# Shifting the start addresses of the low rows of a split-precision transformer block in on-chip memory

## The chip, the cores and the metric

The kernel runs on one core of a Trainium2 chip. A core has five engines that run their own instruction streams and meet at semaphores: TensorE (PE, matrix products; its weight loads are the rows PEld), VectorE (DVE), ScalarE (ACT), GpSimd (POOL) and SyncE (SP), which issues the transfers here. Operands lie in the on-chip memory as 128 partitions by a number of bytes; an address below is the byte offset inside every partition. Products go to eight accumulation banks (PS). The metric is the device time of one execution in microseconds (us), median of several.

## The reference, cut to what matters

Two layers of a hybrid block over 256 tokens `x` and, in layer 0 alone for the outputs, 256 context tokens. Width is 1024, feed-forward width 2816, everything float32.

```python
for l in range(DEPTH):
    # h, hc: x and context after rmsnorm and modulation
    p = h @ w_in[l]; pc = hc @ w_in[l]          # 13 parts: conv a, q k v, recurrent, conv d, gates
    ys = (short_conv(..) @ w_a_out, window_attention(..) @ w_b_out,
          (gelu(r_g) * rglru(..)) @ w_c_out, conformer_conv(..) @ w_d_out)
    x = x + gt1 * (sum(sigmoid(gl) * ys) @ w_out)
    gate, up = split(modulate(rmsnorm(x)) @ w_ffn_in)
    x = x + gt2 * ((silu(gate) * up) @ w_ffn_out)
    # the context tokens go the same way in layer 0 alone
return rmsnorm(x) * g_final
```

## The kernel before

**Split operands.** Nearly every product is made of three. A float32 matrix is held as a rounded part (type fp32r) and a low part (what the rounding left out). For each weight tile of 128x128 and each row tile of activations the helper `products` makes rounded weight times rounded row, rounded weight times low row, and low weight times rounded row, into one bank. So a third of the products stream a low row, and two of three load a rounded weight.

**Where things lie.** `build` allocates one tensor after another with `sb`, each starting at a multiple of 32 bytes. Rounded weights are WH and low weights WL (two slabs each, eight pairs of tiles in a slab). There are two pairs of row tensors. HH and HL (rounded and low) hold the normed input of the block, and later the hidden rows that the second feed-forward product reads (`H` and `FZ` in the code). ZH and ZL hold the branch values of the block (`Z`), and the normed input of the first feed-forward product (`FH`). A row tile k of 512 tokens begins at k * 2048 bytes; 8 * 516 words are reserved for HH and HL, because the helper `unscaled_slab` keeps rows of 258 columns in them, which begin at k * 2064 bytes plus 1032 for the second set of tokens. Of the small tensors, SG and SM hold softmax statistics, AMP, SELB, LC and BD2 small vectors. RAW receives the weight slabs from memory; S, CD, TMP, G and PADA are working rows, and SR, TMPR and PADAR are the same bytes as S, TMP and PADA with the rounded type (the attention uses them).

Bytes modulo 256 at which the tensors begin before: X, WH, WL, ZH, ZL, HH and HL at 0; S, CD, RAW, TMP and G at 128; PADA at 0.

**Order of the work.** Stages follow `STAGES`: c_in, kv, q, d_in, c_out, b_out, a_cu, a_b, a_out, d_out, w_out, and then three times ff_in and ff_out. In each, TensorE takes slabs in turn (`slab`), each once its low weight is made, and its bank pair is emptied. In layer 0 a product has 512 columns, in layer 1 mostly 256. SyncE loads a slab to RAW, ScalarE rounds it to WH, and GpSimd (some by VectorE) subtracts to WL. The instruction before each product loads its own 128x128 tile as weights, also where the same tile was just used.

```python
            def products(s, t, z, w, k, nk=KC):
                zh, zl, at = z
                out = bank(2 * s + t, w)
                a = s * SLAB + k * 2 * P + t * P
                wh, wl = WH[:, a:a + P], WL[:, a:a + P]
                mm(out, wh, row(zh, k, w, at), k == 0, False)
                mm(out, wh, row(zl, k, w, at), False, False)
                return mm(out, wl, row(zh, k, w, at), False, k == nk - 1)
```

Of the kernel before, what the change touches and what calls it, by code (L numbers as in the profile page):

```python
# [24 lines left out]
KC = D // P  # L25
# [144 lines left out]
def build(nc, stream, modw, lruw, xT, cT, prm, rope, consts, outT):  # L170
    with ExitStack() as ctx:
        def sb(name, n, dt=F32):
            return ctx.enter_context(nc.sbuf_tensor(name, [P, n], dt))
# [11 lines left out]
        WH = sb("WH", 2 * SLAB, F32R)  # L185
        WL = sb("WL", 2 * SLAB, F32R)
        ZH = sb("ZH", KC * NT, F32R)
        ZL = sb("ZL", KC * NT, F32R)
        HH = sb("HH", KC * UROW, F32R)
        AMP = sb("AMP", 2 * 2 * KC)  # L190
        SELB = sb("SELB", 32)
        LC = sb("LC", 2 * 16)
        HL = sb("HL", KC * UROW, F32R)
        S, SR = sb_and_rounded("S", KC * NT)
        CD = sb("CD", KC * NT)
# [6 lines left out]
        CST = sb("CST", 5 * P + 2)  # L202
        CIN = sb("CIN", 2 * KC)
        SILC = sb("SILC", 32 * KC + 30)
        SG = sb("SG", 2 * KC)
        LT = sb("LT", 5 * 16)
        EPST = sb("EPST", 2)
        WARM = sb("WARM", 1)
        BD2 = sb("BD2", KC)
        SM = sb("SM", 3 * 14)  # L210
        PS = ctx.enter_context(nc.psum_tensor("PS", [P, 8, 512], F32))

        HB = LT[:, 32:64]
# [5 lines left out]
        def tmp(i, a=0, b=NT):  # L219
            return TMP[:, i * NT + a:i * NT + b]  # L220
# [23 lines left out]
        def lru(n, j, w=NT):  # L244

            if n == KC - 1 and j in (0, 2):
                return row(CD, KC - 2 + j // 2, w)
            return (ALT[j] if n % 2 else S[:, j * NT:(j + 1) * NT])[:, 0:w]
# [9 lines left out]
        def par(l, name, i=0, n=1):  # L258

            return PRM[:, ds(i + (l * NPRM + _cols[name]), n)] if not isinstance(i, int) else \  # L260
                PRM[:, l * NPRM + _cols[name] + i:l * NPRM + _cols[name] + i + n]

        def row(t, j, w=NT, a=0):

            return t[:, j * NT + a:j * NT + a + w] if isinstance(j, int) else t[:, ds(j * NT + a, w)]

        def urow(t, k, c, w=NX, a=0):

            at = k * UROW + c * (NX + 2) + a
            return t[:, at:at + w]  # L270
# [9 lines left out]
        def ubank(t, c, w=NX, a=0):  # L280

            return PS[:, ((4, 6), (5, 1))[t][c], a:a + w]
# [9 lines left out]
        def normed(nm):  # L292
            return (HH, HL) if nm == "n1" else (ZH, ZL)

        def lc(j, n, d):

            return LC[:, ds(n + (16 * j + 8 * d), 1)]

# [4 lines left out]
        def bank(b, w=NT, a=0):  # L303
            return PS[:, b, a:a + w]

        def seqs(ap, c):

            return ap.rearrange("p (c t) -> p c t", c=c)
# [281 lines left out]
        def _(pe):  # L590
            def mm(out, lhs, rhs, start, stop):
                return nc.tensor.matmul(out, lhs, rhs, start=start, stop=stop)  # L592
# [102 lines left out]
            def mod_columns(q, size, out):  # L695

                pe.wait_ge(mod_copied, q + 1)
                for t in range(2):
                    last = mm(out[:, :, 2 * t:2 * t + 2], MROW[q % 2][:, t * P:(t + 1) * P], SELB[:, 0:2 * size], True, True)
                last.then_inc(mod_cols, 1)  # L700

            def unit_columns(j):
# [4 lines left out]
                for g in range(4):  # L707
                    last = nc.tensor.matmul(PS[32 * g:32 * g + 32, 4, 0:n // 4], SELB[:, 0:32],
                                            ACROSS[:, at:at + n].rearrange("p (x g) -> p g x", g=4)[:, g],
                                            start=True, stop=True, tile_position=(0, 32 * g))  # L710
                last.then_inc(mod_cols, 1)

            H, Z, Z2 = (HH, HL, 0), (ZH, ZL, 0), (ZH, ZL, NX)
            FH, FZ = (ZH, ZL, 0), (HH, HL, 0)

            def unscaled_slab(m, l):
# [4 lines left out]
                for k in range(KC):  # L721
# [5 lines left out]
                    for t in range(2):  # L727
                        wh, wl = weights_of(0, t, k)
                        for c in vectors:
                            out = ubank(t, c, NX + 2)  # L730
                            mm(out, wh, urow(HH, k, c, NX + 2), k == 0, False)
                            mm(out, wh, urow(HL, k, c, NX + 2), False, False)
                            last = mm(out, wl, urow(HH, k, c, NX + 2), False, k == KC - 1)
                        if k == KC - 1:
# [104 lines left out]
            for l in range(DEPTH):  # L839
# [30 lines left out]
                for c in range(NT // P):  # L870
                    out = PS[:, 2 + c // 2, (c % 2) * 2 * P:(c % 2 + 1) * 2 * P]
                    for k in range(KC):
                        w0 = SLAB + k * 2 * P
                        h0 = k * NT + c * P
                        mm(out, HH[:, h0:h0 + P], WH[:, w0:w0 + 2 * P], k == 0, False)
                        mm(out, HH[:, h0:h0 + P], WL[:, w0:w0 + 2 * P], False, False)
# [144 lines left out]
        def _(act):  # L1021
            def fn(out, in_, f, **kw):
                return nc.scalar.activation(out, in_, f, **kw)  # L1023
# [8 lines left out]
            def tiles(m, s, t=1):  # L1032
                act.wait_ge(tile_done[s], 2 * m + (t + 1))
# [134 lines left out]
            act.wait_ge(in_loaded, 16)  # L1168
            fn(SG[:, :], CIN[:, :], ACT.Sigmoid).then_inc(sigmoid_c, 1)
            act.wait_ge(par_loaded, 32)  # L1170
# [14 lines left out]
            for l in range(DEPTH):  # L1185
# [50 lines left out]
                def z_high(n):  # L1236
                    act.wait_ge(a["ci_r"].sem, a["ci_r"].at(n, "y"))
                    fn(row(ZH, n, W), lru(n, 5, W), ACT.Copy).then_inc(a["ci_h"].sem, 1)

# [44 lines left out]
                def gate(which, at=0):  # L1284
                    def body(n, s, m):
                        fn(tmp(at + s, 0, W), bank(2 * s, W), ACT.Sigmoid).then_inc(a[which + "_a"].sem, 1)
                    return body
# [36 lines left out]
                def probs(n, u):  # L1324
                    sm = 14 * u
                    act.wait_ge(dv.sem, dv.at(n, f"n{u}"))
                    if u < 2:
                        fn(seqs(bank(4 + u), 2) if l and n == 0 else PR[u], seqs(bank(4 + u), 2), ACT.Exp, scale=SCALE, bias=SM[:, sm + 4:sm + 5],
                           accum_out=SM[:, sm + 6:sm + 7]).then_inc(da.sem, 1)
                    else:  # L1330
                        for q in range(2):
                            fn(PR[0][:, q], bank(6, NC, q * NC), ACT.Exp, scale=SCALE,
                               bias=SM[:, sm + 4 + q:sm + 5 + q], accum_out=SM[:, sm + 6 + q:sm + 7 + q]).then_inc(da.sem, 1)
                    act.wait_ge(dv.sem, dv.at(n, f"f{u}"))
                    q = 2 if u == 2 else 1
                    fn(SM[:, sm + 8:sm + 8 + q], SM[:, sm + 8:sm + 8 + q], ACT.Exp).then_inc(da.sem, 1)

# [47 lines left out]
                if l:  # L1385
                    b = pair_base(l, "c_out")
                    act.wait_ge(a["di_z"].sem, a["di_z"].at(KC - 1, "z"))
                    for n in range(KC):
# [4 lines left out]
                        gate("co")(n, s, m)  # L1393
                        fn(row(ZH, n, W, NX), row(CD, n, W), ACT.Copy).then_inc(a["bz_h"].sem, 1)
                else:
# [7 lines left out]
                    for k in range(KC):  # L1403
                        fn(row(ZH, k, W), row(CD, k, W), ACT.Copy).then_inc(a["bz_h"].sem, 1)
                    tiles(b, 1)
# [101 lines left out]
                for f in range(len(FF_PARTS)):  # L1507
# [7 lines left out]
                    def unscaled_in(m):  # L1515
                        tiles(m, 0)
                        for c in range(C):
                            ue = a["un_e"]
                            act.wait_ge(ue.sem, ue.at(0, f"r0{c}"))
                            last = fn(tmp(0, c * NX, (c + 1) * NX), ubank(0, c), ACT.Sigmoid, bias=SM[:, c:c + 1])  # L1520
                        last.then_inc(fa.sem, 1)
# [16 lines left out]
        def _(dve):  # L1538
            V = nc.vector

            def tt(out, x, y, op):
                return V.tensor_tensor(out, x, y, op)  # L1542
# [4 lines left out]
            def ts(out, x, s1, s2, op0, op1=None):  # L1547
                return V.tensor_scalar(out, x, s1, s2, op0, op1) if op1 is not None else V.tensor_scalar(out, x, s1, None, op0)  # L1548
# [86 lines left out]

            def z_low(n, w, src, at=0, zh=ZH, zl=ZL):
                return tt(row(zl, n, w, at), src, row(zh, n, w, at).bitcast(F32), SUB)

            def decay_rates(l):
# [22 lines left out]
                for j, f in enumerate((-4.0, 2.0)):  # L1662
                    ts(LC[:, 16 * j:16 * j + 16], k0, f, None, MUL).then_inc(lv.sem, 1)
                ts(HB, par(l, "ba", 0, 32), 0.5, None, MUL).then_inc(lv.sem, 1)
# [7 lines left out]
            tt(SILC[:, 30:30 + 32 * KC].rearrange("p (k c) -> p k c", c=32)[:, :, 0:2], CIN[:, :].rearrange("p (k c) -> p k c", c=2),  # L1672
               SG[:, :].rearrange("p (k c) -> p k c", c=2), MUL).then_inc(silu_c, 1)
            dve.wait_ge(par_loaded, 32)
            for g in range(1, 4):
                if g > 1:
                    dve.wait_ge(sel_sum, g - 1)
                tt(SELB[:, :], SELB[:, :] if g > 1 else IDENT[:, 0:32], IDENT[:, 32 * g:32 * g + 32], ADD)\
                    .then_inc(*((silu_c, 1) if g == 3 else (sel_sum, 1)))
            for l in range(DEPTH):  # L1680
# [21 lines left out]

                ts(BD2[:, :], par(l, "conv_d_b", 0, KC), 2.0, None, MUL).then_inc(mv.sem, 1)
                def inverse_root(nm, c_all):
# [270 lines left out]
                def scalars(u):  # L1975
                    q = 2 if u == 2 else 1
                    return (SM[:, 14 * u + 2 * j:14 * u + 2 * j + q] for j in range(7))

# [87 lines left out]
                def conv_d(taps):  # L2066

                    sv = a["cd"].sem
                    for i, k in taps:
                        for t in range(2):  # L2070
# [6 lines left out]
                            if k == 0:  # L2077
                                ins = ts(out, padded(j, C, -(TAPS_D // 2)), w, BD2[:, j:j + 1], MUL, ADD)
                            else:
# [66 lines left out]
                for n in range(KC // 2):  # L2146
# [12 lines left out]
                    else:  # L2159
                        dve.wait_ge(a["ac_v"].sem, a["ac_v"].at(2 * n + 1, "zl"))  # L2160
                        for t in range(2):
                            tt(tmp(2 * s + t, 0, W), row(ZH, 2 * n + t, W).bitcast(F32), row(ZL, 2 * n + t, W).bitcast(F32), ADD)\
                                .then_inc(sv.sem, 1)
# [332 lines left out]
```

## Time and profile before

| | value |
|---|---|
| median of 3 runs | 1960.27 us (1960.24 to 1960.73) |
| profiled execution | 1960.5 us, of which the span of the instructions is 1958.7 us |
| TensorE products | 1930.0 us busy, 99% of the span, 11006 instructions |
| weight loads | 1671.1 us, 85% |
| VectorE, ScalarE, GpSimd | 72%, 46%, 41% |
| memory | 276.25 MB, 141 GB/s on average |

A product's row gives its start and how long it was in the engine. Products overlap, so the pace of TensorE is the distance from one start to the next, not the duration. A weight load shows as a row of its own under PEld, and belongs to the product that starts after it.

### The profile page before, as it was taken

To read this page: it belongs to the slowest core of one execution; us is meant where nothing else is said; L and a number is where in the kernel's file an instruction comes from. 1 tells how busy PE (TensorE), PEld (TensorE's weight loads), DVE (VectorE), ACT (ScalarE), POOL (GpSimd) and SP (SyncE) were. 2 spreads that over 40 slices of the span, in tenths; PEclk is the share of its full clock that TensorE was granted. 3 is DMA by queue.
4 is the path that set the end of the run, shared out by engine and by line. 5 is a ranking of instruction groups with operands and counts; after the bars stand their busy time and mean duration, and the time that the engine had idled before them with its cause. 6 is when DMAs were issued, how large, how long until landed. Compare 5 with 4: busy or idle time off the path is not lost.

```text
span 1958.7 us, 29316 instructions
## 1 busy us (share of the span) xinstructions
PE 1930.0 (99%) x11006; PEld 1671.1 (85%) x11006; DVE 1416.5 (72%) x2475; ACT 908.0 (46%) x1439; POOL 812.0 (41%) x353
## 2 busy tenths in 40 slices
PE   7999999999999999999999999999999999999998
PEld 5778888888888888887888888878899999999998
DVE  5896666677789868798885544689788787645455
ACT  5787544232223343345222223599854435565443
POOL 1002322344444444344344444301647886454432
PEclk9999999999999999999999999999999999999999
DMA  8222211222232235534455442322334554544543
GB/s 344 86 86 81 92 65 65 85 88 107 86 105 88 100 138 216 192 129 170 174 219 192 190 175 83 140 78 106 130 108 151 180 186 174 193 172 172 194 174 127
DMA packets 38701, 276.25 MB, mean 141 GB/s; under 512 B 4416, under 2 KB 4416, under 8 KB 6336
## 3 DMA queue, kind: packets, MB, share of 16 engines
q1 hardware_dynamic: 38592, 274.77, 38.2%
q8 instruction: 72, 1.18, 0.2%
q14 instruction: 37, 0.30, 0.1%
HBM read 273.70 MB, written 1.05 MB: 140 GB/s over the span
## 4 chain that ended last, share of the span: by engine, by line
PE 81%; DVE 13%; ACT 3%; issue 2%; DMA 0%; POOL 0%; SPq 0%; DVEq 0%; ACTq 0%; POOLq 0%
PE PS L592 80%; DVE PS L1545 3%; DVE TMP L1542 1%; DVE TMP L1545 1%; ACT WH L1023 1%; DVE TMP L1548 1%; PE PS L905 1%; DVE S L1545 1%; ACT PS L1023 1%; DVE PS L1542 1%; DVE SM L1991 1%; DVE HL L1545 0%; DVE TMP L1864 0%; DVE ZL L1542 0%; DVE WL L1542 0%
## 5 line engine op out<-in xcount | busy, mean ns | idle before, releaser
L535 POOL TENSOR_TENSOR WL<-RAW,WH 128x1024 fp32r<-128x1024 f32 (+1 forms) x337 | 802.8, 2400 | 1122.9 <-ACT WH L1023 1122.9
L1023 ACT ACTIVATE WH<-RAW 128x1024 fp32r<-128x1024 f32 (+1 forms) x416 | 414.4, 1043 | 606.0 <-PE PS L592 571.4
L592 PE MATMUL PS<-HH,WH 128*128 128x512 f32 (+2 forms) x1968 | 680.7, 346 | 7.3 <-POOL WL L535 3.2
L592 PE MATMUL PS<-HH,WL 128*128 128x512 f32 (+2 forms) x1968 | 667.5, 339 | 0.0
L592 PE MATMUL PS<-HL,WH 128*128 128x512 f32 (+2 forms) x1968 | 666.9, 340 | 0.3 <-DVE HL L1545 0.3
L592 PE MATMUL PS<-ZH,WH 128*128 128x512 f32 (+1 forms) x1312 | 442.1, 337 | 3.7 <-DVE HL L1542 2.9
L592 PE MATMUL PS<-ZH,WL 128*128 128x512 f32 (+1 forms) x1312 | 441.0, 336 | 0.0
L592 PE MATMUL PS<-ZL,WH 128*128 128x512 f32 (+1 forms) x1312 | 439.3, 337 | 0.3 <-POOL ZL L559 0.3
L592 PEld LDWEIGHTS PS<-HH,WH 128*128 128x128 f32 x1968 | 373.0, 190 | 55.8 <-issue 8.2
L592 PEld LDWEIGHTS PS<-HL,WH 128*128 128x128 f32 x1968 | 372.6, 190 | 44.0 <-issue 3.8
L592 PEld LDWEIGHTS PS<-HH,WL 128*128 128x128 f32 x1968 | 373.0, 190 | 41.3
L592 PEld LDWEIGHTS PS<-ZH,WH 128*128 128x128 f32 x1312 | 249.3, 190 | 31.3 <-issue 4.3
L592 PEld LDWEIGHTS PS<-ZH,WL 128*128 128x128 f32 x1312 | 249.5, 190 | 25.7
L592 PEld LDWEIGHTS PS<-ZL,WH 128*128 128x128 f32 x1312 | 248.8, 190 | 26.5 <-DVE ZL L1545 0.7
L1545 DVE SCALAR_TENSOR_TENSOR PS<-G,PRM,PS 128x512 f32<-128x512 f32 (+1 forms) x464 | 254.2, 613 | 0.1
L1542 DVE TENSOR_TENSOR TMP<-TMP,PS 128x512 f32<-128x512 f32 (+1 forms) x54 | 30.3, 562 | 131.7 <-ACT TMP L1023 119.7
L1542 DVE TENSOR_TENSOR WL<-RAW,WH 128x1024 fp32r<-128x1024 f32 (+1 forms) x79 | 113.8, 1457 | 14.4 <-ACT WH L1023 14.4
L1542 DVE TENSOR_TENSOR PS<-TMP,PS 128x256 f32<-128x256 f32 (+1 forms) x86 | 47.6, 555 | 79.2 <-ACT TMP L1023 68.0
L1023 ACT ACTIVATE TMP<-PS 128x256 f32<-128x256 f32 (+1 forms) x144 | 67.9, 471 | 48.1 <-PE PS L592 47.0
L1545 DVE SCALAR_TENSOR_TENSOR PS<-G,SILC,PS 128x512 f32<-128x512 f32 x112 | 84.7, 756 | 4.0
L1545 DVE SCALAR_TENSOR_TENSOR PS<-CD,SILC,PS 128x512 f32<-128x512 f32 x112 | 84.7, 756 | 4.0
L1545 DVE SCALAR_TENSOR_TENSOR X<-PS,MOD,X 128x256 f32<-128x256 f32 (+1 forms) x96 | 41.0, 477 | 38.5 <-PE PS L592 38.3
(210 smaller groups left out, 1740.3 us busy)
## 6 DMA issues: line engine op xcount, KB each, us to landing
RAW<-in_stream SPq DMA_DIRECT2D x200, 1024.0 KB, 4.8
CD<-in_modw SPq DMA_DIRECT2D x22, 1024.0 KB, 7.1
G<-in_modw SPq DMA_DIRECT2D x22, 1024.0 KB, 6.9
RAW<-in_stream SPq DMA_DIRECT2D x8, 768.0 KB, 4.2
CD<-in_lruw SPq DMA_DIRECT2D x2, 2048.0 KB, 11.7
X<-in_xT SPq DMA_DIRECT2D x2, 1024.0 KB, 7.1
S<-in_modw SPq DMA_DIRECT2D x2, 1024.0 KB, 12.9
RAW<-in_modw SPq DMA_DIRECT2D x1, 1024.0 KB, 19.8
```

The lines of the kernel that those rows point to most:

```text
L535: nc.gpsimd.tensor_tensor(WL[:, a:b], RAW[:, a:b], WH[:, a:b].bitcast(F32), ALU.subtract)\
L592: return nc.tensor.matmul(out, lhs, rhs, start=start, stop=stop)
L905: last = nc.tensor.transpose(bank(4 + u, P, q * P), PR[u % 2][:, q // 2, (q % 2) * P:(q % 2 + 1) * P], IDENT)
L1023: return nc.scalar.activation(out, in_, f, **kw)
L1542: return V.tensor_tensor(out, x, y, op)
L1545: return V.scalar_tensor_tensor(out, x, sc, y, op0, op1)
L1548: return V.tensor_scalar(out, x, s1, s2, op0, op1) if op1 is not None else V.tensor_scalar(out, x, s1, None, op0)
L1991: step(V.reduce_max(mx, bank(4 + u), AX.X), f"m{u}")
```

## The change

The tensors keep their sizes, and no instruction is added, removed or moved. Only the order of the allocations is another, and with it the addresses. SG (64 bytes) goes between ZH and ZL. SM (168 bytes, which with rounding up takes 192) goes behind ZL. BD2 (32 bytes) takes the place of SELB and LC (128 bytes each) between HH and HL; SELB and LC go where SG was.

Bytes modulo 256 after: X, WH, WL, ZH and HH stay at 0. ZL begins at 64 and HL at 32. S, CD, RAW, TMP and G begin at 160 instead of 128, PADA at 32 instead of 0. SR, TMPR and PADAR go with theirs.

```diff
         ZH = sb("ZH", KC * NT, F32R)
+        SG = sb("SG", 2 * KC)
         ZL = sb("ZL", KC * NT, F32R)
+        SM = sb("SM", 3 * 14)
         HH = sb("HH", KC * UROW, F32R)
         AMP = sb("AMP", 2 * 2 * KC)
-        SELB = sb("SELB", 32)
-        LC = sb("LC", 2 * 16)
+        BD2 = sb("BD2", KC)
         HL = sb("HL", KC * UROW, F32R)
         S, SR = sb_and_rounded("S", KC * NT)
         CD = sb("CD", KC * NT)
@@
         SILC = sb("SILC", 32 * KC + 30)
-        SG = sb("SG", 2 * KC)
+        SELB = sb("SELB", 32)
+        LC = sb("LC", 2 * 16)
         LT = sb("LT", 5 * 16)
         EPST = sb("EPST", 2)
         WARM = sb("WARM", 1)
-        BD2 = sb("BD2", KC)
-        SM = sb("SM", 3 * 14)
```

## Rows read from the trace of the kernel before

**Rows 1.** The page: busy time of each engine, with its 40 slices and the clock.

```profile
PE 1930.0 (99%) x11006; PEld 1671.1 (85%) x11006; DVE 1416.5 (72%) x2475; ACT 908.0 (46%) x1439; POOL 812.0 (41%) x353
PE   7999999999999999999999999999999999999998
PEclk9999999999999999999999999999999999999999
```

**Rows 2.** Groups by line and form: out<-in, shape, xcount | busy, mean ns | idle before.

```profile
L592 PE MATMUL PS<-HL,WH 128*128 128x512 f32 x1040 | 405.7, 390 | 0.3 <-DVE HL L1545 0.3
...
L592 PE MATMUL PS<-ZL,WH 128*128 128x512 f32 x656 | 254.8, 390 | 0.3 <-POOL ZL L559 0.3
...
L592 PE MATMUL PS<-HL,WH 128*128 128x256 f32 x880 | 248.9, 283 | 0.0
...
L592 PE MATMUL PS<-ZL,WH 128*128 128x256 f32 x656 | 184.5, 283 | 0.0
...
L592 PE MATMUL PS<-HL,WH 128*128 128x258 f32 x48 | 13.5, 282 | 0.0
```

**Rows 3.** Timeline of 457.8 to 460 us, TensorE alone: start us, us, engine.

```profile
457.83 0.39 PE L592 MATMUL PS<-HL,WH 128*128 128x512 f32 x1
...
458.28 0.39 PE L592 MATMUL PS<-HH,WH 128*128 128x512 f32 x1
458.29 0.19 PEld L592 LDWEIGHTS PS<-HL,WH 128*128 128x128 f32 x1
458.51 0.39 PE L592 MATMUL PS<-HL,WH 128*128 128x512 f32 x1
458.51 0.19 PEld L592 LDWEIGHTS PS<-HH,WL 128*128 128x128 f32 x1
...
459.87 0.39 PE L592 MATMUL PS<-HL,WH 128*128 128x512 f32 x1
```

**Rows 4.** The chain that ended last, long pieces: start us, us, what, xcount.

```profile
971.30 239.59 PE PS L592 x1056
...
1474.75 193.92 PE PS L592 x1612
```

**Rows 5.** Timeline of 1600 to 1601.3 us, first and last row (13 starts).

```profile
1599.73 0.28 PE L592 MATMUL PS<-HL,WH 128*128 128x256 f32 x1
...
1601.29 0.28 PE L592 MATMUL PS<-HH,WL 128*128 128x256 f32 x1
```

**Rows 6.** Timeline of 70.9 to 75.5 us, one group of float32 products; mean from groups.

```profile
71.23 3.60 PE L592 MATMUL PS<-TMP,CD 128*128 128x512 f32 x8
...
L592 PE MATMUL PS<-TMP,CD 128*128 128x512 f32 x128 | 57.5, 592 | 0.0
```

**Rows 7.** Timeline of 289 to 298 us: split products after a group of another kind.

```profile
291.81 0.60 PE L905 MATMUL PS<-CST,G 128*128 128x128 f32 x4
292.17 0.48 PE L592 MATMUL PS<-HH,WH 128*128 128x512 f32 x1
292.48 0.39 PE L592 MATMUL PS<-HL,WH 128*128 128x512 f32 x1
292.71 0.39 PE L592 MATMUL PS<-HH,WL 128*128 128x512 f32 x1
292.94 0.40 PE L592 MATMUL PS<-HH,WH 128*128 128x512 f32 x1
...
294.33 1.12 PE L592 MATMUL PS<-TMPR,SR 128*128 128x256 f32 x8
```

**Rows 8.** Timeline of 875.2 to 889.5 us, rows of 258 columns.

```profile
875.28 0.28 PE L592 MATMUL PS<-HH,WH 128*128 128x258 f32 x1
...
875.99 0.28 PE L592 MATMUL PS<-HH,WH 128*128 128x258 f32 x1
...
882.95 0.28 PE L592 MATMUL PS<-HL,WH 128*128 128x258 f32 x1
...
889.34 0.40 PE L592 MATMUL PS<-ZH,WH 128*128 128x512 f32 x1
```

**Rows 9.** The chain's shares by engine, from the page.

```profile
PE 81%; DVE 13%; ACT 3%; issue 2%; DMA 0%; POOL 0%; SPq 0%; DVEq 0%; ACTq 0%; POOLq 0%
```

**Rows 10.** Groups on the other engines that read or write a moved tensor.

```profile
L535 POOL TENSOR_TENSOR WL<-RAW,WH 128x1024 fp32r<-128x1024 f32 (+1 forms) x337 | 802.8, 2400 | 1122.9 <-ACT WH L1023 1122.9
L1542 DVE TENSOR_TENSOR HL<-PS,HH 128x512 fp32r<-128x512 f32 x22 | 15.2, 692 | 15.9 <-ACT HH L1023 15.9
L1542 DVE TENSOR_TENSOR ZL<-TMP,ZH 128x512 fp32r<-128x512 f32 x20 | 13.4, 685 | 6.5 <-ACT ZH L1023 6.5
```

## The prediction

> **What bounds the kernel now.** I read the busy shares first [rows 1]. [...] The next engine, VectorE, is busy for 72%. Then the groups by form [rows 2]: they are what the change can touch, and how many there are. Products that stream a low row of 512 columns are 1040 + 656 = 1696, of 256 columns 880 + 656 = 1536, and of 258 columns 48: 3280 in all. Each stands beside one product of the same shape that streams the rounded row with the same weight, and one with the low weight, so there are 9840 of the kind.
>
> A busy share hides the pace, so the third view is the timeline, where the reader should subtract starts and not look at durations. In the steady part of layer 0 the starts go from 457.83 to 459.87 us in nine steps, 226.7 ns each [rows 3]. Over a long piece of the chain it is the same: 239.59 us over 1056 products is 226.9 ns [rows 4]. In layer 1 thirteen steps take 1.56 us, 120.0 ns each [rows 5], and 193.92 us over 1612 give 120.3 ns [rows 4]. [...]
>
> The same timeline shows what runs at that moment. The load of the next weights starts within 10 ns of the start of a product [rows 3]. So two reads go side by side for the length of the load, one of the moving row and one of the weight tile, and before the change both begin at 0 modulo 256 bytes, for the rounded row as for the low one.
>
> **The change part by part.** *The starts of the low rows.* 3280 products now begin 32 (HL) or 64 (ZL) bytes away from the phase of the weights that are loaded beside them; 1968 of them lie in HL (1040 + 880 + 48) and 1312 in ZL [rows 2]. The other 6560 products keep the phase 0 and differ only in what ran before them. No row before shows a steady run with a low row beside its rounded row at another phase, so the price is bounded from both sides. The lower end is that the low product drops all of its 10.3 ns: 3280 x 10.3 = 33.8 us less. If the product behind it gained as much, it would be 67.6 us. I take neither as likely: the nearest row with other phases is the run of 258 columns, whose rows begin at k * 2064 bytes and so take other phases modulo 256 (rounded and low alike). There six starts at the first row tile take 0.71 us, 118.3 ns [rows 8], and 53 starts over all eight row tiles take 6.39 us, 120.6 ns [rows 8]. [...] The upper end comes from the runs that were disturbed. After a group of another kind, eight split products start between 292.48 and 294.33 us, 231.3 ns each [rows 7], which is 4.6 ns above the steady pace, at unchanged addresses. Whatever keeps the steady pace is therefore a state that a product inherits from the one before it, and can be lost.
>
> The value I take for a low product is half of the 10.3 ns, 5.2 ns: this is the middle between nothing and all of it, and no row is nearer to one end. 3280 x 5.2 = 17.1 us. The chain lies on TensorE for 81% and on VectorE for 13% [rows 9]; where another engine sets the end of a stage, a product that starts earlier only waits longer. Most products lie in the stretches where TensorE is in the chain, so I leave a tenth to waits: 17.1 x 0.9 = 15.4 us.
>
> *The other tensors.* S, CD, RAW, TMP and G move by 32 bytes modulo 256, which meets every slab that ScalarE rounds and GpSimd subtracts. GpSimd takes 2400 ns for half a slab, 337 times, and idles 1122.9 us before them [rows 10], so even a tenth more on each (81 us in all) lies inside its idle time. If that cover were gone, a stage would wait for its low weights by some 0.2 us a half slab. VectorE writes HL or ZL in 692 and 685 ns a row of 512 columns [rows 10], at the same phase for the two today; I cost their new phases at nothing, with 28% of its time free [rows 1], and up to 1 us either way for the pieces on the chain. The attention's products read SR and TMPR, whose phases move together, and PADAR, whose distance to SR stays 128 bytes: nothing, or within 1 us with the disturbed ones.
>
> *The small tensors.* AMP, SELB, LC, SG, SM and BD2 are read a few words at a time; their new homes cost nothing. What is computed, the waits and the transfers are the same.
>
> Sum: 1960.5 us for the profiled execution (its span of 1958.7 and 1.8 us around it) less 15.4 us is 1945.1. The profiled execution lies 0.2 us above the median of 1960.27, so the forecast is 1945.
>
> [...]
>
> **The rivals.** *Nothing happens.* [...] Time: 1960. This is also the case in which the change doesn't do what it says, because the phases that matter are others than modulo 256.
>
> *The steady state is lost: slower.* The steady pace of 226.7 ns is reached after some ten products at one phase for all. If every low row breaks the phase, the low product and the one behind it run at the disturbed pace of 231.3 ns. In 512 columns that is 2 x 1696 x 4.6 ns = 15.6 us; in 256 columns the disturbed paces lie at 118.3 to 120.6 ns for 258 columns [rows 8], so nothing is lost there. Time: 1960.3 + 15.6 = 1976; with the low product alone 1968, with all three 1984. It decides from the point where the state doesn't settle within the three products of a tile. For it: the eight starts [rows 7] show how long a disturbance lasts. Against it: there the disturbance is also a change of kind, type and length, not 32 bytes.
>
> *A large gain.* The low product and the one behind it both lose most of the 10.3 ns: 6560 x 7 = 46 us, 1914. [...]
>
> **How the numbers follow.** Faster as forecast, by 4 to 34 us: 0.40. The large gain: 0.06. Nothing: 0.21. Slower: 0.33. About 0.2% (4 us) is what a measurement of this kernel can tell from no change. So faster 0.46, same 0.21, slower 0.33. The likeliest case's own range is 1926 to 1956. As both signs hold much of the chance, the whole range goes from 1915, at the large gain, to 1980, between the two larger values of the slower case.
>
> **What would show each step right or wrong.** Right: in the stretch of [rows 3] the start distance of low products, or of those behind them, is under 226.7 ns with the three of a tile no longer alike, and the same in the stretch of [rows 5]; GpSimd's 2400 ns and VectorE's 692 and 685 ns stay. If HL at 32 and ZL at 64 differ, the stretches whose products read only one pair show it, each with its own distance. Wrong: distances still at 226.7 and 120.0 (nothing), or all over 226.7 in layer 0 (the lost state). It would also be wrong if the pace fell and the span didn't, which would show as idle time of TensorE at the ends of stages, released by VectorE or GpSimd.

## The result

The changed kernel takes 1977.15 us (median of 3 runs, 1975.13 to 1978.36) against 1960.27 us before: 1.0085 times as long, 95% interval 1.0069 to 1.0100. It is slower by 16.9 us. The profiled execution took 1975.13 us, with a span of 1973.3 us: 14.6 us more than the span before.

The page after, busy time of each engine, answers to [rows 1]:

```profile
PE 1946.5 (99%) x11006; PEld 1664.5 (84%) x11006; DVE 1416.2 (72%) x2475; ACT 908.7 (46%) x1439; POOL 812.0 (41%) x353
PEclk9999999999999999999999999999999999999999
```

Only TensorE has more busy time, by 16.5 us; the other engines stand within a microsecond, with the same counts. The granted clock is 1.00 of full speed in nearly all of the span, as before (mean of the span 0.997 before). It is 0.50 in two stretches of 3.4 us before (from 915.6 and 1246.7 us on) and 0.50 or 0.51 in three after (from 23.5, 928.0 and 1269.3 us on), and low again in the last microseconds (0.50 before, 0.60 after); in the pieces and stretches that are compared below it is 1.00, here and in the experiments. The groups of GpSimd and VectorE that meet the moved tensors show it one by one; of GpSimd's half slabs, against [rows 10]:

```profile
L535 POOL TENSOR_TENSOR WL<-RAW,WH 128x1024 fp32r<-128x1024 f32 (+1 forms) x337 | 802.9, 2401 | 1138.4 <-ACT WH L1023 1138.3
```

Its duration is the same to a nanosecond (2401 against 2400), and it idles 15.5 us longer, which it spends waiting for the rounded weights of ScalarE (`<-ACT WH`).

Where the time went can be read from the chain that ended last. Its long pieces are TensorE alone (start us, us, what, number of instructions). First some of those of before that [rows 4] leave out, then those of after:

```profile
45.86 177.80 PE PS L592 x772
...
1680.35 63.61 PE PS L592 x528
...
1777.06 148.72 PE PS L592 x1236
```

```profile
45.75 180.90 PE PS L592 x772
349.38 472.07 PE PS L592 x2035
...
985.84 244.95 PE PS L592 x1056
...
1494.96 190.64 PE PS L592 x1612
1697.29 62.89 PE PS L592 x528
...
1793.28 147.46 PE PS L592 x1236
```

The reader should subtract the starts of like pieces. The piece of 1056 products, in the feed-forward part of layer 0, starts 14.5 us later than before (985.84 against 971.30) and is itself 5.4 us longer. The piece of 1612, in layer 1, starts 20.2 us later (1494.96 against 1474.75) and is 3.3 us shorter. The piece of 1236 starts 16.2 us later and is 1.3 us shorter, and at the end 14.6 us are left. So the 512-column products of layer 0 cost some 20 us and the 256-column products of layer 1 give more than 5 us back.

The pace itself is read on TensorE's timeline. Here are four stretches, each by its first and last product: 13 steps of c_in in layer 0; then 151 steps in its ff_out (reading HH and HL), 171 steps in ff_out of layer 1 and 166 in its ff_in (reading ZH and ZL).

```profile
64.09 0.40 PE L592 MATMUL PS<-HL,WH 128*128 128x512 f32 x1
...
67.12 0.39 PE L592 MATMUL PS<-HH,WL 128*128 128x512 f32 x1
...
1120.02 0.40 PE L592 MATMUL PS<-HH,WH 128*128 128x512 f32 x1
...
1154.99 0.40 PE L592 MATMUL PS<-HL,WH 128*128 128x512 f32 x1
...
1820.95 0.28 PE L592 MATMUL PS<-HH,WL 128*128 128x256 f32 x1
...
1840.98 0.28 PE L592 MATMUL PS<-HH,WL 128*128 128x256 f32 x1
...
1850.03 0.28 PE L592 MATMUL PS<-ZH,WH 128*128 128x256 f32 x1
...
1869.95 0.28 PE L592 MATMUL PS<-ZL,WH 128*128 128x256 f32 x1
```

They give 233.1 ns and 231.6 ns a step with 512 columns, against 226.7 [rows 3]; and with 256 columns 117.1 ns where HL is read and 120.0 where ZL is, against 120.0 before ([rows 5] for HL; for ZL, 185 steps of the same ff_in, from 1827.69 to 1849.89 us). The extra time isn't the same for each product of a triple (the three products of one weight tile and one row tile): in the first ff_out of layer 0, from 985.76 us on, the next start comes 236.7 ns after a product that streams HL, and 226.0 ns after the one with the low weight. So the figures here are means over triples.

### The profile page after: what moved, and what is told of

Read it like the earlier page. It is cut to its first block, busy times and chain, and to the rows that moved or that the text cites. A ratio compares the mean times of both kernels' runs of the same rounds, so it can differ in the third digit from the quotient of the medians.

```text
span 1973.3 us, 29316 instructions
## 1 busy us (share of the span) xinstructions
PE 1946.5 (99%) x11006; PEld 1664.5 (84%) x11006; DVE 1416.2 (72%) x2475; ACT 908.7 (46%) x1439; POOL 812.0 (41%) x353
## 4 chain that ended last, share of the span: by engine, by line
PE 83%; DVE 10%; ACT 3%; issue 2%; DMA 1%; POOL 1%; SPq 0%; DVEq 0%; POOLq 0%; ACTq 0%
PE PS L592 81%; DVE PS L1545 1%; ACT WH L1023 1%; DVE TMP L1545 1%; PE PS L905 1%; DMA CD<-in_modw 1%; DVE TMP L1548 1%; ACT PS L1023 1%; DVE PS L1542 1%; POOL WL L535 1%; DVE WL L1542 1%; DVE SM L1991 0%; DVE S L1545 0%; DVE TMP L1864 0%; ACT TMP L1023 0%
## 5 line engine op out<-in xcount | busy, mean ns | idle before, releaser
L535 POOL TENSOR_TENSOR WL<-RAW,WH 128x1024 fp32r<-128x1024 f32 (+1 forms) x337 | 802.9, 2401 | 1138.4 <-ACT WH L1023 1138.3
```

The costliest lines, as they stand in the source:

```text
L535: nc.gpsimd.tensor_tensor(WL[:, a:b], RAW[:, a:b], WH[:, a:b].bitcast(F32), ALU.subtract)\
```

## The experiments

Each kernel below is the one before with the edit shown. A pad is a tensor that nobody uses. Each ran beside the kernel before on the same chip, in four sets on four chips, and its ratio is against the runs of its own set. For each, the pieces of its chain that answer to the 1056 products of layer 0 (239.59 us before) and, as far as it is one piece, to the 1236 of layer 1 (148.72 us before) are shown: they hold the same feed-forward work, so their lengths compare the paces directly. Line numbers such as L594 are those of the edited kernels.

### Which address matters

**The other tensors alone.**

```diff
         HL = sb("HL", KC * UROW, F32R)
+        PAD0 = sb("PAD0", 8)
         S, SR = sb_and_rounded("S", KC * NT)
```

> The kernel before with 32 bytes put in behind HL. Rounded and low rows all stay at 0 modulo 256; S, CD, RAW, TMP and G go to 160 and PADA to 32, as in the changed kernel. Theory (the low rows' starts make the loss): 1960 within 2 us, steady starts still 226.7 ns apart in layer 0 and 120.0 ns in layer 1. Rival (the 32 bytes on RAW, S, CD, TMP and G make it, by slower writers or readers): about 1977, with starts at 231 to 233 ns.

Measured: 1960.92 us, ratio 1.0003 (0.9993 to 1.0013).

```profile
971.74 239.60 PE PS L593 x1056
...
1776.13 148.60 PE PS L593 x1236
```

The pieces are as before. RAW, S, CD, TMP, G and PADA at new phases cost nothing that the time shows.

**HL alone at 32, and ZL alone at 64.**

```diff
+        PAD0 = sb("PAD0", 8)
         HL = sb("HL", KC * UROW, F32R)
+        PAD1 = sb("PAD1", 56)
```

> The kernel before with HL alone at 32 modulo 256; ZL at 0, and everything behind HL back at its old place modulo 256. Theory (each low row disturbs the products of its own tile): the triples that read HL go to 232 to 233 ns with 512 columns and to 117 with 256, those that read ZL stay at 226.7 and 120.0. From the changed kernel's pace, 3120 x 5.5 ns more and 2640 x 2.5 ns less: 17.2 - 6.6 = +10.6 us, 1971. Rival (the loss needs two different offsets in turn, 32 and 64): steady paces come back, 1960 to 1963.

Measured: 1971.94 us, ratio 1.0064 (1.0047 to 1.0081).

```profile
979.93 241.40 PE PS L594 x1056
...
1787.57 148.58 PE PS L594 x1236
```

```diff
+        PAD0 = sb("PAD0", 16)
         ZL = sb("ZL", KC * NT, F32R)
+        PAD1 = sb("PAD1", 48)
```

> The kernel before with ZL alone at 64 modulo 256, HL at 0, and everything behind ZL back at its old place modulo 256. Theory: triples that read ZL go to about 231 ns with 512 columns (1968 x 4.5 ns = +8.9 us) and to about 119.5 with 256 (1968 x 0.5 = -1 us): 1968; those that read HL stay at 226.7 and 120.0. Rival (32 bytes is what hurts, 64 is another half of the same line and harmless): 1960 to 1962.

Measured: 1965.87 us, ratio 1.0029 (1.0016 to 1.0042).

```profile
977.07 243.19 PE PS L594 x1056
...
1784.61 147.20 PE PS L594 x1236
```

The two parts cost 11.2 and 5.1 us against the runs beside them, 16.3 together, where both at once cost 16.9. In the piece of layer 0 they add 1.8 and 3.6 us, and the changed kernel adds 5.4: each low row slows the products of its own row pair only. With its 16 and 48 words of pad the second kernel also puts HH and HL another 256 bytes from the weights, and their triples keep 120.0 ns (191 steps from 1812.05 us on); so 256 bytes more made no difference. The forecasts of 1971 and 1968 hold within 2.2 us, but one part of them failed. With 256 columns I expected 117 ns for HL and 119.5 for ZL. The timelines of layer 1 say the reverse; first HL alone in ff_out, 166 steps, then ZL alone in ff_in, 170 steps:

```profile
1815.98 0.28 PE L594 MATMUL PS<-HH,WL 128*128 128x256 f32 x1
...
1835.90 0.28 PE L594 MATMUL PS<-HH,WH 128*128 128x256 f32 x1
```

```profile
1839.93 0.28 PE L594 MATMUL PS<-ZH,WL 128*128 128x256 f32 x1
...
1859.95 0.28 PE L594 MATMUL PS<-ZL,WH 128*128 128x256 f32 x1
```

These are 120.0 ns for HL at 32 and 117.8 ns for ZL at 64, while in the changed kernel, with both, the same stretches had 117.1 and 120.0. For ZL the four tensors concerned (WH, WL, ZH, ZL) lie at the very same addresses in the two kernels. And the kernel with HL alone has both paces in one trace: in stage kv of layer 1 its triples of HL take 47 steps of 117.0 ns.

```profile
1382.40 0.28 PE L594 MATMUL PS<-HH,WH 128*128 128x256 f32 x1
...
1387.90 0.28 PE L594 MATMUL PS<-HH,WL 128*128 128x256 f32 x1
```

So with 256 columns one set of addresses can run at two paces. What chooses between them is not shown. With 512 columns the long stretches of HL's triples took 231.6 ns or more in the two kernels that had HL at 32 and its weights and HH at 0.

### Row against row, or row against weights

**All rows at 32.**

```diff
+        PAD0 = sb("PAD0", 8)
         ZH = sb("ZH", KC * NT, F32R)
@@
         HL = sb("HL", KC * UROW, F32R)
+        PAD1 = sb("PAD1", 56)
```

> The kernel before with ZH, ZL, HH and HL all at 32 modulo 256, weights at 0, the tensors behind HL at their old places. Rounded and low rows are at one phase again, 32 bytes from the weights'. Theory A (what counts is that one streamed row follows another at the same phase): 1960 within 2 us, 226.7 and 120.0 ns. Theory B (what counts is the streamed row's phase against the weight tile that is loaded beside it): all three products of a triple change, so the effect of the changed kernel is there in every product, 1977 or more, and the rounded-row products change too.

Measured: 1974.75 us, ratio 1.0074 (1.0057 to 1.0091).

```profile
990.71 246.59 PE PS L594 x1056
...
1796.65 145.57 PE PS L594 x1236
```

Theory A falls. Rounded and low rows are at one phase again, and the piece of layer 0 is 7.0 us longer, more than in the changed kernel; per product 246.59 / 1056 = 233.5 ns. The piece of layer 1 is 3.2 us shorter, 117.8 ns. The time itself is 2 us under the 1977 that theory B gave as its least.

**The low weights alone at 32.**

```diff
+        PAD0 = sb("PAD0", 8)
         WL = sb("WL", 2 * SLAB, F32R)
+        PAD1 = sb("PAD1", 56)
```

> The kernel before with the low weights WL alone at 32 modulo 256; WH and all rows at 0, everything behind WL at its old place. The load that runs beside a product is that of the next one, so the low weights are loaded while the low row streams, and one product in three gets another distance between streamed row and loaded weights (minus 32), as with a low row at 32 (plus 32). Theory B (distance between the streamed row and the weight tile loaded beside it): steady paces are lost here too, 512 columns at 229 to 233 ns, 256 columns off 120.0; 1970 within 6 us. Rival (only the rows' own phase counts, whatever the weights'): 226.7 and 120.0 ns, 1960.

Measured: 1981.02 us (2 runs), ratio 1.0104 (1.0075 to 1.0133), 5 us over the upper edge of what I gave it.

```profile
989.77 246.59 PE PS L594 x1056
...
1797.81 146.55 PE PS L594 x1236
```

No row has moved here, and the loss in layer 0 is as large as with all rows moved, although only every third load has a new phase. So the weights' address counts as much as the rows'. One load in three is enough to slow the triple, though not evenly: in the ff_in that starts at 1034.60 us, a low row takes 239.8 ns until the next start (the low weights are loaded beside it), the rounded row with the low weight 228.0 and the one with the rounded weight 232.2.

**Everything at 32.**

```diff
         X = sb("X", KC * NT)
+        PAD0 = sb("PAD0", 8)
         WH = sb("WH", 2 * SLAB, F32R)
@@
         HL = sb("HL", KC * UROW, F32R)
+        PAD1 = sb("PAD1", 56)
```

> The kernel before with WH, WL, ZH, ZL, HH and HL all at 32 modulo 256, X at 0, the tensors behind HL at their old places. No operand is at a multiple of 256 or 64 bytes any more, but rows and weights are at distance 0 again. If the distance between the streamed row and the loaded weights sets the pace: 226.7 and 120.0 ns, 1960 within 2 us. Rival (each operand's own place counts, a start inside a 64-byte piece costs more): 233 and 117 ns as with the rows alone at 32, or other paces; 1970 or more.

Measured: 1960.89 us, ratio 0.9998 (0.9988 to 1.0008).

```profile
972.42 239.61 PE PS L594 x1056
...
1778.51 148.59 PE PS L594 x1236
```

Rows and weights are at no multiple of 256 or 64 any more, and both pieces have their old lengths. So what counts is the distance between the streamed row and the loaded weights. That weights "stay on multiples of 256" is of no worth in itself.

### How the pace goes with the distance

**All rows at 64, at 128 and at 224.** The edit is that of the rows at 32, with pads of 16 and 48, 32 and 32, 56 and 8 words.

> The kernel before with all four row tensors at 64 modulo 256, weights at 0. Theory B: every product changes as with all rows at 32 (233.3 ns and 117.2 ns there), by another amount: 230 to 234 ns with 512 columns, under 119.5 with 256; 1967 to 1980. Rival (the two reads meet in pieces of 64 bytes, so that 64 is as good as 0): 226.7 and 120.0 ns, 1960.

> The kernel before with all four row tensors at 128 modulo 256, weights at 0. Theory B with a period of 256 bytes: another pair of paces, 512 columns over 228 ns; by the attention's steps before the change, where PADAR stands 128 bytes from SR, 256 columns at 119 to 122 ns. 1965 to 1985. Rival (the period is 128 bytes or less): 226.7 and 120.0 ns, 1960.

> The kernel before with all four row tensors at 224 modulo 256, 32 bytes ahead of the weights' phase. Theory B, if only the size of the distance counts: as with rows at 32, 233 and 117 ns, 1975. If its sign counts: other paces, to be read from the trace; a pace of 226.7 or less with 512 columns together with less than 120 for 256 would make a faster kernel, under 1958.

Measured: 1960.96 us for 64 (ratio 0.9999, 0.9987 to 1.0010), 1975.40 for 128 (2 runs; 1.0075, 1.0046 to 1.0104) and 1979.76 for 224 (2 runs; 1.0097, 1.0068 to 1.0127). The pieces of 64 and then of 128:

```profile
976.69 241.91 PE PS L594 x1056
...
1779.92 145.86 PE PS L594 x1236
```

```profile
985.47 245.59 PE PS L594 x1056
...
1793.25 146.95 PE PS L594 x1236
```

At 64 my time of 1967 to 1980 is missed. The time is that of before, as the rival has it, but not for its reason: layer 0 loses 2.3 us in this piece and layer 1 gains 2.9, and over the kernel they cancel. At 128 the forecast holds. A distance of minus 32 (224) costs the same 246.59 us in the first piece as plus 32, and gains a little less with 256 columns: 118.3 ns a step in the ff_in that starts at 1848.43 us, where plus 32 has 117.8. The times of the two don't tell them apart, as their intervals overlap.

Per product, from these pieces (layer 0, layer 1): distance 0: 226.9 and 120.3 ns; 32: 233.5 and 117.8; 64: 229.1 and 118.0; 128: 232.6 and 118.9. Of these four, 0 is the best for 512 columns and the worst for 256.

### A kernel that uses it

Layer 0 has 512 columns and wants distance 0, layer 1 has 256 columns and wants 32 or 64. The rows can stay; the weight slabs of layer 1 are put elsewhere, from stage q on.

```diff
-        WH = sb("WH", 2 * SLAB, F32R)
-        WL = sb("WL", 2 * SLAB, F32R)
+        WH = sb("WH", 2 * SLAB + 64, F32R)
+        WL = sb("WL", 2 * SLAB + 64, F32R)
...
+        def home(s, moved):
+            return s * SLAB + 56 if moved else s * (SLAB + 64)
...
-                a = s * SLAB + k * 2 * P + t * P
+                a = home(s, moved[0]) + k * 2 * P + t * P
```

ScalarE, GpSimd and VectorE write their halves to the same homes. 56 words are 224 bytes: distance plus 32. With 48 it is 64, with 40 it is 96.

> Layer 0, and c_in and kv of layer 1, as before (distance 0). From stage q of layer 1 on the weight slabs start 32 bytes in front of a multiple of 256 (224 modulo 256), the rows stay at 0: distance plus 32, as with all rows at 32, where 256 columns take 117.2 ns and not 120.0. The slabs are 256 bytes further apart for it; work and waits are the same. Theory: the 512-column paces stay at 226.7 and about 4400 products of 256 columns gain 2.7 ns each: 11.9 us, 1949. If VectorE, which sets the end of some pieces in layer 1, keeps a third of it: 1953. Rival (the pace at a distance was a property of moved rows, not of distance): 1960.

> The same with the weight slabs of layer 1 (from stage q on) at 192 modulo 256: distance plus 64, where 256 columns took 117.8 ns in a regular cycle. Theory: 4400 x 2.2 ns = 9.7 us, 1951; less what VectorE keeps, up to 1954. Rival as in the kernel with 32: 1960.

> The same as the two kernels with moved weights in layer 1, now at 160 modulo 256: distance plus 96, which no run has shown. If the gain with 256 columns falls steadily with the distance (2.7 ns at 32, 2.2 at 64, 1.2 at 128, all against 120.0): about 1.7 ns, 118.3 ns a start, 1953 to 1955. If 64 bytes is the unit in which the two reads meet and 96 is 32 again: 117.0 ns and 1951.

Measured: 1951.62 us for 32 (5 runs, ratio 0.9952, 0.9939 to 0.9966); 1953.45 for 64 (5 runs, 0.9962, 0.9948 to 0.9975); 1960.66 for 96 (0.9999, 0.9989 to 1.0009). The kernel with 32, its piece of layer 0 and the two that layer 1's 1236 have become:

```profile
971.61 239.59 PE PS L601 x1056
...
1770.38 21.27 PE PS L601 x180
1791.72 123.46 PE PS L601 x1056
```

Layer 0 is untouched, and in layer 1 a product takes 123.46 / 1056 = 116.9 ns. This kernel beats both: it is 9.0 us (0.5%) under the 1960.62 of the kernel before that ran beside it, and some 25 under the changed one. I expected 1949 to 1953 and 1951 to 1954, so both hold. The kernel with 96 is a miss: I expected 1951 to 1955, by a trend over three distances, and its piece of layer 1 has the old length:

```profile
972.15 239.59 PE PS L601 x1056
...
1778.79 148.60 PE PS L601 x1236
```

So the gain doesn't fall steadily with the distance, and 96 isn't 32 again. The kernel with 96 has the same edit but for one number, so the gain of the other two comes from the distance and not from the slabs being further apart. At distance 32, though, the moved weights gave 116.9 ns where moved rows gave 117.8 over their piece. The trace with moved rows has a stretch of 116.7 too (191 steps from 1752.12 us on), so this is again two paces at one distance.

## Why the prediction was wrong

**What bounds the kernel.** Right in the main. TensorE's pace sets the time, of 9840 products of one kind, and addresses move that pace: in the piece of 1056 products of 512 columns it is 226.9 ns a product before and 233.5 with all rows at 32. Nothing else took part that the runs show: the kernel with the other tensors moved alone is at 1.0003, and GpSimd's half slab at 2401 ns. The granted clock is not at its upper level throughout, as said above, without harm to the argument. And the eight float32 rows of [rows 6] are four products of the program (`gates` issues four), each recorded as two rows, (3.60 - 0.592) / 7 = 429.7 ns from one start to the next.

**The value taken for a low product.** This is the step that failed, by its sign. I took half of 10.3 ns as a gain, the middle of the interval, as "no row is nearer to one end". The 10.3 ns were my estimate, and no run shows them as a part of a product that addresses can take off; the 33.8 and 67.6 us and the large gain are counted from them. What the runs showed in their place, against 226.9 and 120.3 ns a product at distance 0: with 512 columns 2.2 to 6.6 ns more at every distance tried, with 256 columns at most 3.4 ns less (116.9). An estimate from the rows compares the costs: a straight line through the two widths, 226.7 and 120.0 ns [rows 3, 5], has 0.417 ns a column and leaves 13.3 ns; one through the float32 rows of 512 columns, 429.7 ns apart [rows 6], and of 128, (0.60 - 0.272) / 3 = 109 ns apart ([rows 7], with the mean of the group of 64), has 0.83 ns a column and leaves 2.5 ns (0 to 5, as the times are rounded to 0.01 us). The row that was nearest I had put under the upper end: 231.3 ns after a disturbance [rows 7]. The changed kernel's triples of HL run at 231.6 and 233.1 ns, that is 4.9 to 6.4 ns more for each of the three products on average, and not 5.2 ns less for one. That 231.3 and 231.6 have one cause is not shown: the first was seen at unchanged addresses. I had reasoned from the size of a cost to the direction of a change in it. That the load runs beside the product doesn't say that distance 0 is where this costs most; for 512 columns it is the best of the distances tried.

**The tenth left to waits.** It was too small as well. The piece of 1056 products lost 5.36 us, 5.1 ns a product; for all 5088 products of 512 columns that would be 25.8 us, an estimate, and some 20 had appeared by the start of the piece of 1612. The rest went into waits or stretches that no piece here shows apart.

**The rival that came.** "The steady state is lost" gave 1976 for two of three products at 4.6 ns, and 1977.15 was measured. Its mechanism holds in part. That one low operand at another distance slows the triple is shown by HL alone and by the low weights alone. But the price was put together wrongly: a triple pays 3 x 4.9 to 3 x 6.4, so 14.7 to 19 ns, and not 2 x 4.6 = 9.2, and with 256 columns the paces don't stay, they fall to 117.1 ns where HL is read. The two errors cancel, so that the 1976 came out is luck. It is also not a state that is lost for good: the new addresses have a regular cycle of their own, at 233.1 ns in c_in, step after step.

**The 118.3 ns of the 258-column rows** [rows 8] was misread. I took it for a pace at other phases, but at the first row tile, k = 0, the rows begin at 0 and at 1032 bytes, which are 0 and 8 modulo 256, and the six starts come right behind products of another width. The rows of all eight tiles begin at 0 to 120 bytes in steps of 8, and they took 120.6 ns, where the straight line through the two widths has 120.8 for 258 columns (120.0 + 2 x 0.417, an estimate). So no row said that other phases take time off. That 256 columns do run at 116.9 to 118.9 ns at several distances came out later, and I had carried the sign over to 512 columns too, which are half of the products and have more than half of the time. Priced apart, with [rows 7] for one width and [rows 8] for the other, the sum would have been slower.

**The load beside the product.** That the next weights are loaded beside the running product [rows 3] does bear on the pace: 1981.02 us was measured with the low weights moved and no row, and 1960.89 with weights and rows moved together. So the time goes with where the loaded weights lie against the streamed row.

**Chances and range.** The slower case had 0.33 and the forecast 0.46. The time lies inside the range, but that took in both signs, so it says little.

**What stays open.** What the two reads share is not shown, only that their distance counts. Why 96 bytes gives nothing with 256 columns, and why the same distance of HL runs at 120.0 ns in one stretch and 117.1 in another, is not settled. Distances that are no multiple of 32 were tried by no experiment; only the 258-column rows have some. Distances of 160 and 192, and 96 with 512 columns, were not tried either. That the pace repeats after 256 bytes rests on the one case of HH and HL above.

## What to carry to other kernels

Where every product loads its own weights, as here with rounded float32 operands, the pace can depend on the distance (here modulo 256 bytes) between the start of the streamed row and that of the weight tile loaded beside it, not on alignment as such: in this kernel 226.9 to 233.5 ns a product with 512 columns, and 116.9 to 120.3 with 256. The best distance differed by width (0 for 512 columns, 32 for 256), so measure each width apart and subtract starts over a hundred steps rather than read durations. A kernel with two widths can give each its own distance for 256 bytes of pad a weight tensor; here that was worth 9.0 us of 1960.62.

## What the runs showed of the hardware

Moving the low weights by 32 bytes, with nothing else changed, made 1.04% of the time; I had not expected that weights' addresses weigh as much as rows'. The paces repeat closely over hundreds of products: the same 246.59 us for 1056 products in three kernels (all rows at 32, all rows at 224, low weights at 32). And with 256 columns there are two steady paces at one set of addresses, 120.0 and 117.0 ns for HL at 32 in one trace. What chooses between them no run shows.
